# Feed-forward stage of a two-block model: order of the modulation pieces, two running sums, a first slice taken by k, five places for down weights

## What is computed

```python
mod = cond @ ada_w[i] + ada_b[i]                       # 6 x 1024 values
hin = x * (1 + sc2) + sh2
gate, up = jnp.split(hin @ ffn_w_in[i], 2, axis=-1)    # 1024 -> 2 x 2816
y = (jax.nn.silu(gate) * up) @ ffn_w_out[i]            # 2816 -> 1024
x = _layernorm(DEEPNORM_ALPHA * x + (1 + gt2) * y, ln_g[i, 1], ln_b[i, 1])
```

## Time and profile before

| | |
|---|---|
| median of three runs | 2822.98 us (2822.43 to 2825.48) |
| the profiled execution, its own time | 2827.32 us |
| its span, first to last instruction | 2825.6 us |
| PE busy | 2593.6 us, 92% of the span |
| DVE busy | 2056.6 us, 73% |
| ACT busy | 981.4 us, 35% |
| mean granted clock of TensorE | 0.958 of full |

### The profile page before, as it was taken

The page is one execution under the profiler, slowest core; times in us unless marked ns, Lnnn a source line. Parts: engine busy times, 40 slices in busy tenths (PEclk is TensorE's granted clock), DMA queues, the critical chain, the costliest instruction groups (busy, mean ns, idle before and its releaser), DMA issues. The chain is left out here.

```text
span 2825.6 us, 43032 instructions
## 1 busy us (share of the span) xinstructions
PE 2593.6 (92%) x17354; PEld 2031.5 (72%) x17354; DVE 2056.6 (73%) x2802; ACT 981.4 (35%) x1057; POOL 393.4 (14%) x211
## 2 busy tenths in 40 slices
PE   5999988879999989998999996999898999999993
PEld 3785988447888754564788875897678788888883
DVE  6872667888776638536877757885865799999994
ACT  2631111122220022432222103343222677777773
POOL 1000000100000020000000000000001266666651
PEclk8999999989999999999999998999998999999997
DMA  5221122336663280202666323232306699999973
GB/s 203 90 69 40 63 78 78 135 111 185 188 178 119 82 271 31 75 31 67 191 186 188 127 97 104 90 90 60 127 22 236 243 367 370 375 368 363 365 304 139
DMA packets 247796, 459.85 MB, mean 163 GB/s; under 512 B 31125, under 2 KB 205869, under 8 KB 232297
## 3 DMA queue, kind: packets, MB, share of 16 engines
q1 hardware_dynamic: 227592, 433.41, 44.1%
q0 software_dynamic: 14384, 24.25, 2.5%
q10 hardware_dynamic: 5682, 0.20, 0.1%
HBM read 457.28 MB, written 30.56 MB: 173 GB/s over the span
## 5 line engine op out<-in xcount | busy, mean ns | idle before, releaser
L49 PE MATMUL ffn_bank<-ffn_xT_high,ffn_wi_high 128*128 128x512 f32 x704 | 281.4, 400 | 11.3 <-DVE ffn_wi_low L43 6.1
L50 PE MATMUL ffn_bank<-ffn_xT_low,ffn_wi_high 128*128 128x512 f32 x704 | 279.2, 397 | 0.0
L415 DVE SCALAR_TENSOR_TENSOR ffn_nsum<-ffn_nw,ffn_cond,ffn_nsum 128x256 f32<-128x256 f32 x336 | 163.0, 485 | 12.0
L49 PEld LDWEIGHTS ffn_bank<-ffn_xT_high,ffn_wi_high 128*128 128x128 f32 x704 | 134.4, 191 | 43.3 <-DVE ffn_wi_low L43 7.2
L3225 POOL DMA_INDIRECT expert_rows<-exp_ys,exp_to_row x32 | 155.6, 4861 | 45.3 <-issue 44.5
L50 PEld LDWEIGHTS ffn_bank<-ffn_xT_low,ffn_wi_high 128*128 128x128 f32 x704 | 134.4, 191 | 28.5
L43 DVE TENSOR_TENSOR moe_u_low<-moe_u,exp_u_high 128x4096 fp32r<-128x4096 f32 x32 | 141.6, 4425 | 12.3 <-ACT exp_u_high L3299 12.3
L43 DVE TENSOR_TENSOR moe_g_low<-moe_g,moe_g_high 128x4096 fp32r<-128x4096 f32 x32 | 141.7, 4428 | 10.6 <-ACT moe_g_high L3299 10.5
L49 PE MATMUL ffn_bank<-ffn_wo_high,ffn_act_high 128*128 128x512 f32 x352 | 137.9, 392 | 5.3 <-DVE ffn_wo_low L43 5.3
L43 DVE TENSOR_TENSOR moe_d_low<-moe_d,exp_d_high 128x4096 fp32r<-128x4096 f32 x32 | 141.4, 4419 | 0.0
L51 PE MATMUL ffn_bank<-ffn_xT_high,ffn_wi_low 128*128 128x512 f32 x352 | 140.5, 399 | 0.0
(11 more groups left out here) (691 smaller groups left out, 6563.9 us busy)
## 6 DMA issues: line engine op xcount, KB each, us to landing
moe_g<-in_w_e_gate SPq DMA_DIRECT2D x32, 2048.0 KB, 9.0
moe_u<-in_w_e_up SPq DMA_DIRECT2D x32, 2048.0 KB, 9.5
moe_d<-in_w_e_down SPq DMA_DIRECT2D x32, 2048.0 KB, 8.6
ffn_nw<-in_ada_w SPq DMA_DIRECT2D x24, 1024.0 KB
ffn_nw<-in_w_ada SPq DMA_DIRECT2D x24, 1024.0 KB
stay_z<-in_ffn_w_in SPq DMA_DIRECT2D x44, 512.0 KB, 5.2
ffn_wi<-in_ffn_w_in SPq DMA_DIRECT2D x44, 512.0 KB, 5.1
ffn_wo<-in_ffn_w_out SPq DMA_DIRECT2D x44, 512.0 KB, 3.4
```

Source lines behind the costliest of these rows:

```text
L49: nc.tensor.matmul(out, w[0], x[0], start=start, stop=False, **kw)
L50: nc.tensor.matmul(out, w[0], x[1], start=False, stop=False, **kw)
L415: nc.vector.scalar_tensor_tensor(out=total, in0=nw[:, b, k, :], scalar=cond[:, k:k + 1], in1=total, op0=ALU.mult, op1=ALU.add).then_inc(s[ ...
```

## The change

- **One piece per half.** Only piece 0 stays ahead of slice 0's `gate_up`. Slices 0 to 5 are written out (`PEELED` = 3 pairs); behind their `gate_up` DVE makes pieces 1, 2, 4, 5, 7 and 8 (`first_piece`), ahead of the `split_in`, and behind the `split_in` of slices 1 and 3 one more each, 3 and 6. PE sums piece p a slice later, and the extra one between the gate and the up part. From slice 6 on the loop has one piece per slice as before, and the last piece, 23, comes after slice 20. SP's loads follow the same order. The scaling of `gt` (before L431) moves from ahead of piece 0 to behind slice 5.
- **Two running sums.** Even k go to `nsum` and odd k to a new tile `nsum_odd`, so that an instruction waits for the one two before it; the bias, now a tile of 128 partitions that is zero outside the first, enters at k = 0, and an addition of both sums stands where the bias was added.
- **First slice by k.** ACT and DVE treat slice 0's gate and up part apart; PE waits for two instead of eight of ACT's parts, and runs for each k the gate and the up part.
- **Five places.** `wo` has five places: one of its own, which SP loads behind slice 5, two in `stay_z`, which can be loaded when slice 20 is through, and two where `ffn_wi` was, loadable when slice 21 is through. `split_out(1)` moves behind the last `gate_up`.
- **Last five by tile and half.** `STEADY` is 17, and in the last part PE goes for each tile and each column half through the five f, instead of for each tile through the four f with both halves.

```diff
--- before.py
+++ after.py
...
 
     PAIRS = NF // 2
     PIECES = NF + 2
-    WO_RING = 4
+    WO_RING = 5
+    PEELED = 3
+    SUMS = KD + 1
     STEADY = NF - WO_RING
     PIECE = 6 * D // PIECES
     gate = mod[5 * D:6 * D]
...
+            down.sb("gap", [P, D])
+            g = down.sb("g", [P, D])
+            b = down.sb("b", [P, D])
+            last_wo = [down.shared((f"wo{i}", [P, D], F32), (f"wo_low{i}", [P, D], F32R)) for i in (3, 4)]
...
+        first_wo = room.shared(("wo0", [P, D], F32), ("wo_low0", [P, D], F32R))
+        mid_wo = [[stay[n][:, i * D:(i + 1) * D] for n in ("z", "z_r")] for i in range(2)]
+        wo, wo_low = zip(*[[half[:, :] for half in slot] for slot in (first_wo, *mid_wo, *last_wo)])
...
+        def first_piece(n):
+
+            return n + 1 + (n > 1) + (n > 3)
...
+                sp.wait_ge(s["nbias_zero"], 1)
                 load_piece(0, 0)
                 load_piece(1, 1)
 
+                def next_load(p, b):
+                    sp.wait_ge(s["nsum_done"], p)
+                    load_piece(p, b)
+
+                def first_half(n):
+                    p = first_piece(n - 1) + 2
+                    next_load(p, p % 2)
+                    sp.wait_ge(s["hidden"], 2 * n + 2)
+                    load_in(n + 2, n % 2)
+                    if n in (2, 4):
+                        next_load(p + 1, (p + 1) % 2)
+
...
-                        if isinstance(i, int):
-                            for b in range(2):
-                                sp.wait_ge(s["nsum_done"], 2 * h + b + 2)
-                                load_piece(2 * h + b + 2, b)
-                        else:
-                            sp.wait_ge(s["nsum_done"], i * 2 + (h + 4))
-                            load_piece(i * 2 + (h + 4), h)
...
+                for n in range(2 * PEELED):
+                    first_half(n)
+                sp.dma_start(wo[0], w_out_v[0]).then_inc(wo_loaded[0], 16)
+                with sp.Fori(PEELED, PAIRS - 1) as i:
                     pair(i)
-                for f in range(NF):
+                for f in range(1, NF):
                     slot = f % WO_RING
-                    if f == 0:
-                        sp.wait_ge(s["nsum_done"], PIECES + 1)
-                    if f == 2:
+                    if f == 1:
+                        sp.wait_ge(s["hidden"], 2 * NF - 2)
+                    elif f == 3:
                         sp.wait_ge(s["hidden"], 2 * NF)
                     if f >= WO_RING:
                         sp.wait_ge(s["down_used"], f - WO_RING + 1)
-                    sp.dma_start(wo[slot][:, :], w_out_v[f]).then_inc(wo_loaded[slot], 16)
+                    sp.dma_start(wo[slot], w_out_v[f]).then_inc(wo_loaded[slot], 16)
...
+                def half(i, h, between=None):
+
+                    pe.wait_ge(s["wi_split"], i * 2 + h + 1)
+                    pe.wait_ge(s["act_done"], i * 2 + h + 1)
+                    for n in range(2):
+                        for k in range(KD):
+                            last = hidden(h, n, k)
+                        last.then_inc(s["hidden"], 1)
+                        if n == 0 and between is not None:
+                            next_sum(between, between % 2)
+
+                pe.wait_ge(s["first_split"], 2)
+                for k in range(KD):
+                    pe.wait_ge(s["xT_split"], k + 1)
+                    for n in range(2):
+                        last = hidden(0, n, k)
+                        if k == KD - 1:
+                            last.then_inc(s["hidden"], 1)
+                for n in range(1, 2 * PEELED):
+                    half(n // 2, n % 2, first_piece(n - 1) - 1 if n % 2 else None)
+                    next_sum(first_piece(n - 1), first_piece(n - 1) % 2)
+                with pe.Fori(PEELED, PAIRS) as i:
...
                 for t in range(NT):
-                    for f in range(STEADY, NF):
-                        if t == 0:
-                            pe.wait_ge(s["wo_split"], f + 1)
-                        down(f, t)
+                    for j in range(NH2):
+                        for f in range(STEADY, NF):
+                            if t == j == 0:
+                                pe.wait_ge(s["wo_split"], f + 1)
+                            down(f, t, j)
...
-                    nc.vector.tensor_scalar(total, nw[:, b, 0, :], cond[:, 0:1], None, ALU.mult).then_inc(s["nsteps"], 1)
-                    for k in range(1, KD):
-                        dve.wait_ge(s["nsteps"], p * KD + k)
-                        nc.vector.scalar_tensor_tensor(out=total, in0=nw[:, b, k, :], scalar=cond[:, k:k + 1], in1=total,
-                                                       op0=ALU.mult, op1=ALU.add).then_inc(s["nsteps"], 1)
-                    dve.wait_ge(s["nsteps"], p * KD + KD)
-                    nc.vector.tensor_tensor(total[0:1, :], total[0:1, :], nbias[:, b, :], ALU.add).then_inc(s["nsum_biased"], 1)
-                    dve.wait_ge(s["nsum_biased"], p + 1)
+                    for k in range(KD):
+                        if k > 1:
+                            dve.wait_ge(s["nsteps"], p * SUMS + k - 1)
+                        if k == 1:
+                            ins = nc.vector.tensor_scalar(nsum_odd[:, :], nw[:, b, k, :], cond[:, k:k + 1], None, ALU.mult)
+                        else:
+                            out = nsum_odd[:, :] if k % 2 else total
+                            ins = nc.vector.scalar_tensor_tensor(out=out, in0=nw[:, b, k, :], scalar=cond[:, k:k + 1],
+                                                                 in1=out if k else nbias[:, b, :], op0=ALU.mult, op1=ALU.add)
+                        ins.then_inc(s["nsteps"], 1)
+                    dve.wait_ge(s["nsteps"], p * SUMS + KD)
+                    nc.vector.tensor_tensor(total, total, nsum_odd[:, :], ALU.add).then_inc(s["nsteps"], 1)
...
-                split_in(0, 0)
+                for n in range(2):
+                    dve.wait_ge(s["first_high"], n + 1)
+                    low_half(nc.vector, wi_low[0][:, n, :, :], wi[0][:, n, :, :], wi_high[0][:, n, :, :]).then_inc(s["first_split"], 1)
+                nc.vector.memset(marks[:, 6:7], 0.0).then_inc(s["wi_split"], 1)
...
+
+                def after_row(p, b):
+                    dve.wait_ge(s["n_psum"], p - 1)
+                    next_piece(p, b)
+
+                for n in range(2 * PEELED):
+                    p = first_piece(n)
+                    gate_up(n, n % 2)
+                    if p == 1:
+                        next_piece(p, 1)
+                    else:
+                        after_row(p, p % 2)
+                    split_in(n + 2, n % 2)
+                    if n in (1, 3):
+                        after_row(p + 1, (p + 1) % 2)
+                dve.wait_ge(s["gt_loaded"], 16)
+                link(nc.vector.tensor_scalar(gt[:, :], gt[:, :], 1.0, None, ALU.add))
...
+                        after_row(i * 2 + (h + 3), 1 - h)
...
                 gate_up(NF - 2, 0)
+                after_row(PIECES - 1, 1)
                 split_out(0)
+                gate_up(NF - 1, 1)
                 split_out(1)
-                gate_up(NF - 1, 1)
```

More of the change, by code:

```diff
@@ L262, in next_sum @@
                     nc.tensor.matmul(bank[4 + b][:, 0:PIECE], ones[:, :], nsum_low[:, b, :], start=False, stop=True).then_inc(s["n_psum"], 1)
-                def pair(i):
-                    for h in range(2):
-                        pe.wait_ge(s["wi_split"], i * 2 + h + 1)
-                        pe.wait_ge(s["act_done"], i * 2 + h + 1)
-                        for n in range(2):
-                            for k in range(KD):
-                                if isinstance(i, int) and h == n == 0:
-                                    pe.wait_ge(s["xT_split"], k + 1)
-                                last = matmul_halves(nc, bank[2 * h + n][:, :], (wi_high[h][:, n, k, :], wi_low[h][:, n, k, :]),
-                                                     (xT_high[:, k, :], xT_low[:, k, :]), start=(k == 0), stop=(k == KD - 1))
-                            last.then_inc(s["hidden"], 1)
-                        if isinstance(i, int):
-                            next_sum(2 * h, 0)
-                            next_sum(2 * h + 1, 1)
-                        else:
-                            next_sum(i * 2 + h + 2, h)
@@ L282, in _, with hidden @@
-                pair(0)
-                with pe.Fori(1, PAIRS) as i:
-                    pair(i)
-                def down(f, t):
-                    toks, slot = slice(t * P, (t + 1) * P), f % WO_RING
-                    for j in range(NH2):
-                        cols = slice(j * HALF, (j + 1) * HALF)
-                        last = matmul_halves(nc, bank[2 * t + j][:, :], (act_high[:, f, toks], act_low[:, f, toks]),
-                                             (wo_high[slot][:, cols], wo_low[slot][:, cols]), start=(f == 0), stop=(f == NF - 1))
-                        if f == NF - 1:
```

(32 more changed lines are left out.)

78 lines of the change are left out of this document (23 added, 55 removed).

## The result

Eight runs of the changed kernel have a median of 2804.74 us; one of them took 4294.4 us at a mean granted clock of 0.563 and is left out of the ratio, and the other seven have a median of 2802.76 us. Eight of the kernel before have 2820.61 us. The ratio is 0.9944, 95% interval 0.9927 to 0.9961: 15.8 us less, 11 to 21, which is under one per cent but clear of the noise. The profiled execution took 2802.76 us (span 2800.9) against 2827.32 before.

What follows compares the result with a forecast made beforehand. The prediction took DVE to bound the start of both feed-forwards and its norm rows the end. Gains of 9.6 and 10.9 us at the starts and 0 at the ends made 20.5 us, from 2822.98 to 2802.5 us, range 2795 to 2811.

Steps and rivals of the forecast that it cites:

- Rival (c): DVE's pieces: two sums save nothing, a piece stays at 5.14 us, 2.5 us lost per feed-forward, 2807.5 us; chance 0.13.
- What is late next: Ahead of slice 2: its load, behind piece 2's, comes late; PE stops 4.0 us, 4.8 in the second feed-forward.
- The clock: Behind PE's stops: half of each stretch at 1.2 GHz is lost, 0 to 3.3 us, taken as 2.3.
- No stop from slice 3 on: Later slices of the start: loads and DVE's work stay hidden, but for some 0.2 us; no stop ahead of slice 3.
- the prediction's own list of what would show it wrong: Slice 2's load far from 8.7 us, stops of 1 to 2 us ahead of later slices, or 1.2 GHz beyond 7 us.
- rival (e): Slices 3 to 7: each load takes 8.74 us, PE stops 1.5 us each, 38 us slower in all, 2841; chance 0.03.
- The end: Last down weights: ready 5.5 us earlier, but the stop grows from 2.63 to 4.0 us; sum 0, bounds -2 and +4.6.

Runs made afterwards that it cites:

- the repeat: The changed kernel run once more, unaltered, to see how far its stages repeat: 2807.54 us, ratio 0.9951 to the kernel before.
- e1_one_sum: The changed kernel with the piece's sum written as one running sum again, the rest kept: 2807.3 us, ratio 0.9947 to the kernel before.
- e3_tail_tile0_by_f: The changed kernel with tile 0 of the last five slices taken by slice with both halves: 2792.32 us, ratio 0.989 to the kernel before.

## Why the prediction was right, and where its sizes were off

It said 20.5 us less from stages; they gave 17.7 (17.6 in the repeat), and whole runs 15.8 (11 to 21). Of the 2.8 us that are missing 0.9 lie in the first start, 0.2 in the middles and 1.8 in the ends, while the second start gave 0.1 more. That the forecast of 2802.5 us lies 2 us from the median is in part luck: it started from 2822.98 us, the median of three runs and 2.4 above that of eight, and this offset half of the 4.7 us by which the 15.8 fell short of the 20.5. What the new order of the pieces gives by itself was not run; the kernel with one sum again, in which it stands beside the other parts, has 12.7 us less in the stages than the kernel before.

**Two running sums.** Right: 0.40 us apart and 4.29 us a piece, taken from projection rows. Rival (c) is ruled out by e1_one_sum: the same piece takes 5.16 us where every step reads the last. Its price was 2.5 us per feed-forward, measured 2.5 and 3.4. The prediction named for it the Trainium skill's VectorE: DVE Perf Modes, "The DRAIN you can't avoid"; that section also says that a next op that is not held (made to wait until all earlier ones are finished) starts earlier, and the trace agrees with that sentence: a step lasts 0.48 us and the next starts after 0.40. The estimate of 0.34 us a step from the Trainium skill's Vector Engine (DVE) Microarchitecture Reference, "Measured stream behaviour on trn2", is too low for these rows: 0.40.

**First slice by k.** PE goes on at 603.5 without a gap, as said. What the prediction did not say, though its sum takes slice 2's start from the load alone, is that this gain goes into the next stop: with it or without it slice 2 starts at 630.1 to 630.3.

**What is late next.** Right in place, chain and size. Slice 2's load was forecast at 617.9 with 8.74 us to the cast and a stop of 4.0 us; it was 617.27, 8.73 and 4.20 (5.14 for 4.8). That the neighbouring load ahead makes it slow is shown: issued first it takes 6.15 and 7.17 us. The start gave 8.7 us for 9.6 forecast, and 11.0 for 10.9.

**The clock.** The term of 2.3 us a stop was of the right size. The stretches at 1.2 GHz behind the stops, in the changed kernel:

```profile
630.00:636.50 6.50, 6.22 (x15) 4.87 (x16) 6.33 (x16) 2.52 (x3) 0.00 (x0) 0.50 0.21 54
961.00:964.25 3.25, 3.25 (x8) 2.58 (x9) 1.38 (x2) 0.00 (x0) 0.00 (x0) 0.52 0.00 0
1336.50:1343.00 6.50, 4.24 (x10) 3.38 (x11) 6.43 (x11) 2.35 (x3) 0.00 (x0) 0.50 0.52 135
1667.50:1674.00 6.50, 4.75 (x11) 3.78 (x12) 3.05 (x4) 0.00 (x0) 0.00 (x0) 0.50 0.00 0
```

Half of the time that PE is busy in them is lost: 3.1, 1.6, 2.1 and 2.4 us, 2.3 on the mean. The 3.1 is 0.8 above the 2.3, which is nearly all of the 0.9 us that the first start lacks.

**No stop from slice 3 on.** Off by a small term: slice 7's load also stands behind a piece's, 1.6 and 1.9 us ahead of it, and takes 8.66 and 9.22 us. The stops are 0.66 and 1.47 us. A stop of 1 to 2 us ahead of a later slice stands in the prediction's own list of what would show it wrong; the 1.47 us is one, at one slice of one feed-forward. It is rival (e) for one slice of five; the loads of slices 3 to 6 took 6.0 to 6.6 us and once 7.6. The first middle became 0.6 us longer, the second 0.4 us shorter.

**The end.** The stop was 3.88 and 4.04 us for 4.0 forecast, DVE ended 5.0 us behind PE for 4.96, and the margin at the start of the down part held: PE is busy for 96.32 of 96.33 us. The two ends became 0.1 and 1.7 us longer, forecast 0 in all. The term that failed is when PE reaches the stop: 5.5 + 1.4 us earlier, said the prediction, and it was 102.20 - 96.33 = 5.9. Two of the five places keep their low half in `stay_z_r`, and there 24 products take 5.55 us; in the place behind them it is 5.47, where only the first products are slower, in the other two 5.44, and before the change always 5.44. PE's first product with a low half, of down slices 1 to 5 of the changed kernel:

```profile
866.37 0.40 PE L50 MATMUL ffn_bank<-stay_z_r,ffn_act_high 128*128 128x512 f32 x1
...
871.92 0.39 PE L50 MATMUL ffn_bank<-stay_z_r,ffn_act_high 128*128 128x512 f32 x1
...
877.47 0.40 PE L50 MATMUL ffn_bank<-ffn_wo_low,ffn_act_high 128*128 128x512 f32 x1
...
882.94 0.39 PE L50 MATMUL ffn_bank<-ffn_wo_low,ffn_act_high 128*128 128x512 f32 x1
...
888.38 0.39 PE L50 MATMUL ffn_bank<-ffn_wo_low,ffn_act_high 128*128 128x512 f32 x1
```

Over 17 slices, seven of them in `stay_z_r`, that comes to 93.35 - 17 x 5.44 = 0.9 of the missing 1.0 us. The clock took 26.69 - 108 x 0.234 = 1.4 us and 2.2 (22.47 / 96 = 0.234 at full clock in e3_tail_tile0_by_f), less than the 2.3 of the sum.
What the prediction did not draw from its own count (12 products ready where it had been 18) is that the order by half is a loss in itself. Over the same five places the old order ends 3.6 and 4.5 us earlier.

## What to carry to other kernels

Gains ahead of a load that is late don't add up: find the next wait and take it out, and only then count the others (in the stages the first slice by k gave nothing with slice 2's load late, 2 to 3 us with it early). Where weights share a queue with small pieces, issue first what is due first; for slice 2 it gave 4 to 5 us a feed-forward here. Look at the next loads then: in one feed-forward slice 5's fell in behind a piece's by it and came 0.7 us late. Before an order is changed where the next operand is due, count the work that can be done until it comes: 12 products fewer cost 2.7 us of stop and the clock behind it.
